# Where the gated one-hots of the gate table are made: two tokens in four on GpSimd, VectorE's row in PSUM

## The reference

```
out[token] = sum over slots of  g[slot] * gelu(h[token] . u[expert(slot)]) * v[expert(slot)]
expert(slot) = 128 * e1[slot] + e2[slot]          (of 16384 experts)
```

```
G[e2, e1, token] = sum over slots of  [e2 == e2[slot]] * [e1 == e1[slot]] * g[slot]
```

## Time and profile before

| | us |
|---|---|
| median of 3 runs (lowest, highest) | 3033.35 (3031.37, 3034.01) |
| the profiled execution, its own time | 3032.16 |
| its span in the trace | 3030.5 |
| gate table stage, first layer, first to last VectorE instruction | 1034.7 to 1127.6 |
| gate table stage, second layer | from 2181.3 |
| TensorE, VectorE, ScalarE, GpSimd busy over the span | 2529.0, 1979.4, 1180.7, 40.1 |

### The profile page before, as it was taken

How to read it: one execution, slowest core, us unless ns; L and a number is a source line. 1 busy time by engine, 2 the same in 40 slices (tenths; PEclk the granted TensorE clock), 3 DMA queues, 4 the chain that set the end, 5 groups by cost and what they waited for, 6 DMA issues and landing times. The chain is left out here.

```text
span 3030.5 us, 44615 instructions
## 1 busy us (share of the span) xinstructions
PE 2529.0 (83%) x13933; PEld 2127.9 (70%) x13933; DVE 1979.4 (65%) x4652; ACT 1180.7 (39%) x2073; POOL 40.1 (1%) x28
## 2 busy tenths in 40 slices
PE   4949794896658379999999997697379999999996
PEld 3747542664537369999999996376368999999995
DVE  4874778555677996666666665376995666666664
ACT  3524302231032384444444443162284444444442
POOL 0000000000000100000000000000100000000000
PEclk9975797558789799999999999799699999999998
DMA  6740472005631005555555554202005555555553
GB/s 225 274 166 1 137 252 97 28 14 194 251 108 52 0 24 191 182 190 182 192 181 191 182 192 148 101 27 72 1 0 188 193 181 190 183 192 182 189 185 111
DMA packets 159076, 428.07 MB, mean 141 GB/s; under 512 B 15348, under 2 KB 21776, under 8 KB 158992
## 3 DMA queue, kind: packets, MB, share of 16 engines
q1 hardware_dynamic: 158992, 427.09, 41.9%
HBM read 426.00 MB, written 1.05 MB: 141 GB/s over the span
## 5 line engine op out<-in xcount | busy, mean ns | idle before, releaser
L2072 ACT ACTIVATE v_high<-v_ring 128x1024 fp32r<-128x1024 f32 x256 | 271.7, 1061 | 345.5 <-PE bank L2017 345.5
L2105 DVE CAST weighted_high<-activated 128x256 fp32r<-128x256 f32 x256 | 75.8, 296 | 473.2 <-PE bank L2017 473.2
L2089 DVE TENSOR_TENSOR u_t_low<-u_ring,u_t_high 128x1024 fp32r<-128x1024 f32 x256 | 312.8, 1222 | 33.4 <-issue 17.0
L2017 PE MATMUL bank<-v_high,weighted_high 128*128 128x512 f32 x1024 | 319.2, 393 | 2.0 <-DVE weighted_low L2107 2.0
L2017 PE MATMUL bank<-v_low,weighted_high 128*128 128x512 f32 x1024 | 317.2, 391 | 0.0
L2017 PE MATMUL bank<-v_high,weighted_low 128*128 128x512 f32 x1024 | 316.3, 390 | 0.0
L2096 DVE TENSOR_TENSOR v_low<-v_ring,v_high 128x1024 fp32r<-128x1024 f32 x256 | 312.0, 1219 | 0.7 <-ACT v_high L2072 0.7
L2007 PEld LDWEIGHTS bank<-h_t_high,u_t_high 128*128 128x128 f32 x2048 | 281.1, 192 | 30.1 <-DVE u_t_low L2089 10.5
L2007 PE MATMUL bank<-h_t_high,u_t_high 128*128 128x256 f32 x2048 | 287.9, 284 | 9.6 <-DVE u_t_low L2089 9.6
L2007 PE MATMUL bank<-h_t_low,u_t_high 128*128 128x256 f32 x2048 | 288.9, 284 | 0.0
L2007 PE MATMUL bank<-h_t_high,u_t_low 128*128 128x256 f32 x2048 | 288.3, 284 | 0.0
(11 more groups left out here) (417 smaller groups left out, 3592.0 us busy)
## 6 DMA issues: line engine op xcount, KB each, us to landing
u_ring<-in_peer_u SPq DMA_DIRECT2D x256, 512.0 KB, 4.4
v_ring<-in_peer_v SPq DMA_DIRECT2D x256, 512.0 KB, 3.6
mod_ring<-in_ada_w SPq DMA_DIRECT2D x96, 512.0 KB, 7.3
panel<-in_l_w_in SPq DMA_DIRECT2D x15, 2048.0 KB, 9.6
panel<-in_peer_w_q SPq DMA_DIRECT2D x8, 2048.0 KB, 8.0
panel<-in_l_w_out SPq DMA_DIRECT2D x4, 2560.0 KB, 9.9
panel<-in_lru_w_in SPq DMA_DIRECT2D x4, 2048.0 KB, 8.1
mod_ring<-in_kv_ada_w SPq DMA_DIRECT2D x16, 512.0 KB, 6.7
```

Of the source, the lines that this page charges most:

```text
L2017: last = nc.tensor.matmul(banks[4 + 2 * t + half][:, :], w[:, t * P:(t + 1) * P], v[:, k, half * 512:(half + 1) * 512], start=False, stop= ...
L2072: nc.scalar.activation(VH[:, s, :], VR[:, s, :], ACT.Copy).then_inc(v_high, 1)
L2089: nc.vector.tensor_tensor(UTL[:, s, :, :].rearrange("p a b -> p (a b)"), UR[:, s, :], UTH[:, s, :, :].rearrange("p a b -> p (a b)").bitcas ...
L2105: nc.vector.tensor_copy(WH[:, :], AA[:, s, :]).then_inc(w_high, 1)
```

## The change

GpSimd makes the gated one-hots of tokens 0 and 1 of each step, in a buffer of its own (`O1P`, 4 KB a partition behind `O1` and `O2`), with the same tensor_scalar that VectorE uses; VectorE makes those of tokens 2 and 3. The plain one-hots and ScalarE's gating are gone, so ScalarE only stores. VectorE first copies the row `iota` into the PSUM bank `banks[4]`, waits for that copy, and reads the row from there in all of its comparisons; GpSimd reads `iota` in SBUF. TensorE waits for `pool_hot` where it waited for `gated`. GpSimd waits for `built` of the step four back like VectorE, and its 64 steps are all written out, not looped.

```diff
-            plain, gated = sem(f"peer{l}_plain_onehots"), sem(f"peer{l}_gated")
-            ACT_TOKENS = 2
+            pool_hot, rows_copied = sem(f"peer{l}_pool_onehots"), sem(f"peer{l}_rows_copied")
+            POOL_TOKENS = 2
...
+        O1P = nc.alloc_sbuf_tensor_at(f"onehot1_pool_{l}", [P, R4, 2, P], F32, offset=PANELS + R4 * 4096)
+            rows = banks[4][:, 0:P]
...
                     def step(n, s):
                         at_least(dve, built, n - R4 + 1)
                         tok = slice(4 * n, 4 * n + 4) if type(n) is int else bass.ds(4 * n, 4)
-                        rows = iota[:, :].unsqueeze(1)
-                        nc.vector.tensor_tensor(O2[:, s, :, :], rows.broadcast_to([P, 4, P]),
+                        nc.vector.tensor_tensor(O2[:, s, :, :], rows.unsqueeze(1).broadcast_to([P, 4, P]),
                                                 slot_e2[:, tok].unsqueeze(2).broadcast_to([P, 4, P]), ALU.is_equal)
-                        tok = slice(4 * n, 4 * n + ACT_TOKENS) if type(n) is int else bass.ds(4 * n, ACT_TOKENS)
-                        nc.vector.tensor_tensor(O1[:, s, 0:ACT_TOKENS, :], rows.broadcast_to([P, ACT_TOKENS, P]),
-                                                slot_e1[:, tok].unsqueeze(2).broadcast_to([P, ACT_TOKENS, P]),
-                                                ALU.is_equal).then_inc(plain, 1)
-                        for u in range(ACT_TOKENS, 4):
-                            tok = slice(4 * n + u, 4 * n + u + 1) if type(n) is int else bass.ds(4 * n + u, 1)
-                            last = nc.vector.tensor_scalar(O1[:, s, u, :], iota[:, :], slot_e1[:, tok], slot_g[:, tok],
-                                                           ALU.is_equal, ALU.mult)
+                        for u in range(POOL_TOKENS, 4):
+                            last = nc.vector.tensor_scalar(O1[:, s, u, :], rows, slot_e1[:, token(n, u)],
+                                                           slot_g[:, token(n, u)], ALU.is_equal, ALU.mult)
                         last.then_inc(hot, 1)
+                    nc.vector.tensor_copy(rows, iota[:, :]).then_inc(rows_copied, 1)
+                    dve.wait_ge(rows_copied, 1)
...
+                @block.gpsimd
+                def _(pool):
+                    def step(n, s):
+                        at_least(pool, built, n - R4 + 1)
+                        for u in range(POOL_TOKENS):
+                            last = nc.gpsimd.tensor_scalar(O1P[:, s, u, :], iota[:, :], slot_e1[:, 4 * n + u:4 * n + u + 1],
+                                                           slot_g[:, 4 * n + u:4 * n + u + 1], ALU.is_equal, ALU.mult)
+                        last.then_inc(pool_hot, 1)
+                    for n in range(S // 4):
+                        step(n, n % R4)
...
-                        pe.wait_ge(gated, n + 1)
+                        pe.wait_ge(pool_hot, n + 1)
...
+                            o1 = O1P if u < POOL_TOKENS else O1
+                            last = nc.tensor.matmul(banks[s][:, u * P:(u + 1) * P], O2[:, s, u, :], o1[:, s, u, :],
...
-                    def gate(n, s):
-                        act.wait_ge(plain, n + 1)
-                        for u in range(ACT_TOKENS):
...
-                            last = nc.scalar.activation(O1[:, s, u, :], O1[:, s, u, :], ACT.Copy, scale=slot_g[:, tok])
-                        last.then_inc(gated, 1)
```

More of the change, by code:

```diff
@@ L1891, in at_least, with token @@
                     eng.wait_ge(s, value)
+            def token(n, u):
+                return slice(4 * n + u, 4 * n + u + 1) if type(n) is int else bass.ds(4 * n + u, 1)
+            rows = banks[4][:, 0:P]
             with StageBlock() as block:
@@ L1920, in step @@
                         pe.wait_ge(hot, n + 1)
-                        pe.wait_ge(gated, n + 1)
+                        pe.wait_ge(pool_hot, n + 1)
                         at_least(pe, stored, n - R4 + 1)
                         for u in range(4):
-                            last = nc.tensor.matmul(banks[s][:, u * P:(u + 1) * P], O2[:, s, u, :], O1[:, s, u, :],
+                            o1 = O1P if u < POOL_TOKENS else O1
+                            last = nc.tensor.matmul(banks[s][:, u * P:(u + 1) * P], O2[:, s, u, :], o1[:, s, u, :],
                                                     start=True, stop=True)
@@ L1946, in store @@
                             .then_inc(stored, 1)
[L1948 to L1951, removed]
+                    for s in range(R4):
+                        store(s, s)
                     with act.Fori(1, S // 16) as i:
                         for s in range(R4):
-                            gate(R4 * i + s, s)
-                            store(R4 * i + s - 1, (s - 1) % R4)
-                    store(S // 4 - 1, R4 - 1)
+                            store(R4 * i + s, s)
         NB = N_KEYS
```

## The result

The changed kernel takes 3048.44 us (median of 6 runs, 3043.88 to 3052.22), the kernel before 3033.68 us (6 runs, 3030.52 to 3035.64). The ratio is 1.0047, with a 95% interval of 1.0035 to 1.006: slower by 11 to 18 us, where 3007 us was forecast. It went the way of the first rival, GpSimd setting the pace, which had been priced at 3046 us for 0.77 us an instruction.

What follows compares the result with a forecast made beforehand. VectorE was taken to bound the gate table stage; (1.450-1.242) x 64 x 2 = 26.6 us saved, less 0.7 us for the row copy, from 3032.16 us, plus 1.2 us to the median, gave 3007 us. Range 2998 to 3050 us.

Steps and rivals of the forecast that it cites:

- the first rival: Gate table stage: GpSimd's two-pointer instruction lasts over 0.725 us and sets the pace; 3046 us at 0.77 us; chance 0.20.
- VectorE bounds the stage, ScalarE's wait is a shadow: Gate table stage before: VectorE sets 1.45 us a step; TensorE's 17.9 us wait for ScalarE comes from VectorE.
- Comparison from PSUM, 0.60 us apart; gated ones 0.321 us each; VectorE's step 1.24 us: VectorE in the changed stage: 128x512 comparison stays at 0.60 us, two gated one-hots take 0.64 us, between 1.11 and 1.51.
- Row copy 0.33 us, tail and barrier unmoved, GpSimd's longer program fetched at no cost: Stage ends: copy and wait add 0.33 us a stage, 0.7 us in all; tail and next loads keep their lengths.
- TensorE's 1.16 us a step as the next bound: TensorE in the stage: a step takes 1.16 us, just under VectorE's 1.24, the bound if VectorE reaches its low end.
- The low end of the range: Whole kernel: time down to 2998 us, with TensorE as the bound.
- Mutual exclusion: Changed stage: VectorE and GpSimd keep each other out, 2.14 us a step, 3122 us; chance 0.05.
- GpSimd takes 0.45 us an instruction, hidden under 1.24: GpSimd's two gated one-hots: 0.90 us a step, covered by VectorE's 1.24 up to 0.62 us each.
- no net change: Changed stage: GpSimd near 0.725 us, or dearer PSUM reads on VectorE, cancel the gain; 3031 us; chance 0.07.

Runs made afterwards that it cites:

- e3: The kernel before, with VectorE reading the row from PSUM instead of SBUF (ScalarE gates two tokens, GpSimd idle): 3046.85 us, ratio 1.0044.
- e5: The changed kernel with GpSimd's compare replaced by a multiply in all steps (two multiplies, its half of the table not one-hot): 3006.83 us, ratio 0.9909.
- e1: The changed kernel with GpSimd's instruction in eight forms, eight steps each, VectorE silent after four steps in the second layer: 2998.52 us, one run.
- e8: Against the kernel before: VectorE makes eight plain one-hots, GpSimd gates three tokens in one two-tensor multiply, ScalarE the fourth: 3007.64 us, ratio 0.9919.
- e2: The changed kernel with VectorE's row read from SBUF in all its instructions, without the row copy: 3092.38 us, ratio 1.0192.
- e9: The changed kernel with eight more forms of GpSimd's instruction (other operations, some with 64 columns), VectorE silent after four second-layer steps: 3002.72 us, one run.

## Why the prediction was wrong

- *VectorE bounds the stage, ScalarE's wait is a shadow:* right. In e3 ScalarE's work is the same and VectorE's step longer, and the whole stage went with VectorE to 1.57 us a step, while TensorE's wait for ScalarE grew. The changed kernel alone doesn't show it, since GpSimd bounds the stage there.
- *Comparison from PSUM, 0.60 us apart; gated ones 0.321 us each; VectorE's step 1.24 us:* right. 690 and 403 ns long in the changed kernel; e3 and e5 show the distances, 1.235 us a step in e5.
- *Row copy 0.33 us, tail and barrier unmoved, GpSimd's longer program fetched at no cost:* right. The copy took 0.33 us, and GpSimd's 128 instructions have no gap. From the last one-hot (GpSimd's, 1140.16 us) to VectorE's first instruction of the next stage (1142.47) lie 2.3 us, where 2.5 us lay before.
- *TensorE's 1.16 us a step as the next bound:* wrong, without harm to the time here. TensorE makes a step in 0.893 us in e1's silent layer. The low end of the range (2998 us, by its own terms 2997) and the fear that TensorE would cap the gain rested on it. In e8 it was VectorE that set 1.195 us.
- *Mutual exclusion (0.05):* did not happen, in the changed kernel; e1's silent layer shows it (790 against 791 ns). e2 shows that the row in PSUM is the reason.
- *GpSimd takes 0.45 us an instruction, hidden under 1.24:* wrong, and the step that failed. It lasts 0.791 us and takes 0.773 us from start to start, 1.547 us a step, so it is not hidden and sets the pace. The base of 0.29 us came from the affine select, the nearest row in shape, and I took its price to be that of any one-input operation of 128 columns. Without pointers, compare and multiply last 0.641 us: 0.35 us more than the base. The two pointers are 0.150 us for the 0.12 of VectorE's price, 0.03 us more. Less the 0.04 us that the forecast had rounded up, that is the 0.34 us between 0.45 and 0.79. Most of it lies in the columns: (646-292)/384 = 0.92 ns each for the affine select, 3.4 ns for compare and multiply, (3.4-0.92) x 128 = 0.32 us. Two multiplies without pointers do last what the affine select does (297 ns); that its price fits them is luck, as they were not what the kernel ran.
- *The rivals:* the one that came true had 0.20. Its mechanism (TensorE waits on pool_hot, VectorE idles on built) is what the waits show, and its price at 0.77 us an instruction was 3046 us for 3048.44 measured. The range reached it; the direction of the forecast was wrong. How it came to 0.77 us is not borne out: compare and multiply were to be several passes over the columns, at the price of the 512-column affine select (0.65 us). By e1 and e9 two multiplies cost less than one (447 against 602 ns), so operations don't add up as passes, and that 0.646 came near 0.641 us is luck. For no net change the prediction had 3031 us; with the 1.2 us between profiled run and median, which its other sums have, it is 3032.

The Trainium skill's rule on small reads, cited ahead ("GPSIMD Engine Reference", section "Performance pitfalls for Q7 kernels"), made 0.085 us a pointer by the prediction's estimate. The runs show 0.075 us, near it, but not whether a pointer is such a read; and the pointers were the smaller part of what was missing.

## What to carry to other kernels

Work moved to an engine that has never run that operation in the trace has no price yet: measure the instruction with its own operations, pointers and columns before you count on cover, since on GpSimd the pair of operations alone moved it from 447 to 790 ns. If GpSimd must help with a gated one-hot, let VectorE compare and let GpSimd multiply several tokens in one wide two-tensor multiply, as e8 does (0.83 us for three); a tensor_scalar that only multiplies is no cheaper there than one that only compares. Beside a GpSimd that sets the pace, let VectorE read one of the inputs of a two-tensor instruction from PSUM. And don't take a step of an engine that other engines feed for its own pace: the earlier trace rows had TensorE at 1.16 us where it can do 0.893.

## What the runs showed of the hardware

- GpSimd's tensor_scalar, 128x128 fp32: two pointers with is_equal, is_ge, subtract or max ahead of a multiply 782 to 792 ns; multiply or add ahead of a multiply 447 or 448; one operation with one pointer 601 or 602 whether it multiplies or compares (e1, e9); 75 ns a pointer ((641 to 791), (525 to 601), (297 to 447)). A single multiply is slower than two.
- VectorE slows GpSimd from 0.773 to 0.978 us an instruction with its row in SBUF (e2) and not at all with it in PSUM (790 against 791 ns, e1), and its own comparison goes from 700 to 705 ns.
- TensorE makes a step of four fp32 products of 128x128x128 in 0.893 us with VectorE silent, at the granted clock 1.00 (e1).
- A PSUM source adds nothing to the distance of VectorE's two-tensor comparisons (0.60 us for 512 columns either way, e3), and to tensor_scalar only the halved column rate: 0.32 for 0.255 us at 128 columns.
